# State-space stage: position-table products nine planner ticks sooner, and each table sent out in eight pieces from SyncE's queue

## The chip, the cores and the metric

The kernel runs on one core of a Trainium2 chip. The metric is the device time of one launch in microseconds (us); the number that counts is the median of the runs. One further execution is profiled, and all rows of the trace come from that one.

## The reference

Two transformer-like blocks over a sequence of 512 positions with 1024 features. The first has a state-space mixer (32 heads in 4 groups, scan in chunks of 128), convolutional feed-forward layers, and a differential attention with a learned bias by distance. The second has three mixed branches (one of them a sliding-window attention with its own bias table), a cross-attention and a feed-forward layer. The parts that the change touches are the two bias tables, which depend on nothing but the parameters:

```python
bias = rel_bias[t5_bucket(dist)].astype(jnp.float32).transpose(2, 0, 1)
logits = logits + bias[None, :, None]                 # first block, 8 heads
...
bias = rel_bias.astype(jnp.float32)[t5_bucket_2(dist)]  # second block, 8 heads
```

and the state-space mixer, beside which they are built:

```python
y_diag = jnp.einsum('bcgls,bgrcls,bcsgrp->bclgrp', cb, decay_in, xc)
states = jnp.einsum('bclgn,bgrcl,bclgrp->bcgrpn', bc, decay_states, xc)
y_off = jnp.einsum('bclgn,bcgrpn,bgrcl->bclgrp', cc, states_in, jnp.exp(a_cs))
```

## The kernel before

**Main work.** Nearly all time is matrix products with features on the partitions: 512 positions are the moving side, blocks of 128x128 weights the stationary one. Each product is made of three passes over a high and a low part (`features`, L1162). A group of output features takes one of the PSUM banks 0 to 2 in turn and is a row of pieces, two chunks of 128 inputs (six matmuls) each.

**The planner.** `Plan` writes the order of everything. One piece of main work is one tick; there are 1598. `self.start(name, key)` notes the tick at which a step begins; each engine's program runs through the ticks and, for each, issues what stands at `T - age`. So an engine's order is fixed; the engines run apart and are held together by semaphores alone. `self.once(name, key, test, windows)` starts a step at the first tick at which `test` holds and `place(windows)` finds banks: a window is (key, age, ticks), and each gets the lowest of the banks 3 to 7 that is free in these ticks. Taking a bank on TensorE (`take`) waits until the bank's former user has been read out.

**Weights.** A unit of 1024 columns (512 KB) is loaded by SyncE (`load`, L2746), split by ScalarE (`split`, the copy 128x1024 of L1562), cut by VectorE (`cut`, L2027, 128x1024), then used by TensorE. There are three buffers (`N_W`), so SyncE's load of a unit waits for the cut of the unit three earlier. In this stage one load is issued every four ticks.

**State-space stage.** For each of four groups `g`: `in` products with a convolution (VectorE's three L2030 of 128x512 each), `sta` (transposes `bt`, scores `scb`), `stb` (transposes `xc(g,c)` at ticks 0 to 3 of it, states `st(g,c)` at 7, 9, 11, two ticks of bank each), and four `pair` steps three ticks apart: `s0`, `s1`, then ScalarE's Relu and Exp on them, GpSimd's product, `bo` and `by`. ScalarE copies `st(g,0)` out one tick after it; `st(g,1)` and `st(g,2)` are added by VectorE. Group 0 has `sta` at tick 30, `stb` at 40, `pair` at 50, 53, 56, 59; group 1 has `stb` at 67 and `pair` from 77. `dec` at tick 19 prepares decays: `d1`, `d2` (bank 3, ticks 26 to 30), `d3` (bank 4, 30 to 32). `yn` of group 0 (tick 86) writes `Y0` over the memory in which the table inputs and tables lie, so it waits until these have gone out.

**The tables.** Rule `tabs`: it starts one tick after the end of `("in", 0, 5)`, tick 29. It makes four products `tb 0` to `tb 3`, five ticks apart (bank windows of five ticks; banks 5, 3, 3, 3), each of 8 rows by 320 columns, the last by 64 (L1271 to L1276). VectorE subtracts each from a mask two ticks later (L2206 to L2210) into `tabs[0]` (`tab1`, 640 columns) and `tabs[1]` (`tab2`, 384 columns), on 8 partitions. ScalarE then issues one DMA for each to HBM (L1671 to L1675), each row 128 times over: 8 x 128 x 640 and 8 x 128 x 384 floats, at ticks 37 and 57. Their readers (`tb` and `tb2`, SyncE) come hundreds of ticks later. Banks otherwise: `xc(0,0..3)` have 4, 5, 6, 7; `st(0,0)` 4, `st(0,1)` 3, `st(0,2)` 3; `st(1,0)`, `st(1,1)`, `st(1,2)` all 3; `s0(0,0)` 4, `s1(0,0)` 5.

Of the kernel before, what the change touches and what calls it, by code (L numbers as in the profile page):

```python
# [17 lines left out]
P = 128  # L18
# [22 lines left out]
L1, L2 = 640, 384  # L41
# [109 lines left out]
FIRST_ROW = 13  # L151
# [3 lines left out]
class Plan:  # L155
# [22 lines left out]
    def at(self, name, t):  # L178
        return self.starts.get(name, {}).get(t, ())
# [182 lines left out]
    def ssm(self):  # L362
# [5 lines left out]
        def first_row():  # L368
            if self.T >= FIRST_ROW and self.when("rms", "n1") is None:
                self.rms("n1")  # L370

        self.rules.append(first_row)
        self.once("tabs", 0, lambda: ("in", 0, 5) in self.end and self.T > self.end["in", 0, 5],
                  [(("tb", i), 5 * i, 5) for i in range(4)])
        self.once("dec", 0, lambda: ("dt",) in self.ev, [(("d1",), 1, 2), (("d2",), 7, 5), (("d3",), 11, 3)])
        silu = {}
# [615 lines left out]
class Kernel:  # L992
# [12 lines left out]
    def full(self, key):  # L1005
        return self.sig.bank[self.plan.bank[key]].full, self.turn(key)

    def empty(self, key):
        return self.sig.bank[self.plan.bank[key]].empty, self.turn(key)
# [545 lines left out]
def scalar_program(eng, K):  # L1555
    plan, buf, sig, dram = K.plan, K.buf, K.sig, K.dram
    at, full, empty, leave = plan.at, K.full, K.empty, K.leave
    w = Waits(eng)
# [83 lines left out]
    def ssm(T):  # L1642
        for key in at("conv", T - 1):
            _, g, i = key
# [10 lines left out]
        for key in at("conv", T - 3):  # L1655
            _, g, i = key
# [6 lines left out]
        for key in at("zsilu", T - 1):  # L1663
            _, g, i = key
# [3 lines left out]
            func(ACT.Tanh, buf.us[plan.u_n[key] % 3][:, 4:S + 4], buf.ZT[g % 2][:, i, :]).then_inc(*sig["tanh"].up(key))  # L1668
        for _ in at("once", T):
            eng.dma_start(buf.once[:, :], dram["once"]).then_inc(*sig.once.up())  # L1670
        for i, (name, ln, age) in enumerate((("tab1", L1, 8), ("tab2", L2, 28))):  # L1671
            for _ in at("tabs", T - age):
                w.wait_ge(*empty(("tb", 2 * i + 1)))
                eng.dma_start(dram[name], buf.tabs[i][:, 0:ln].unsqueeze(1).to_broadcast([8, P, ln])).then_inc(
                    *sig.tabs[i].up())  # L1675
        for _ in at("dec", T - 3):
            w.wait_ge(*sig["absn"].at())
            eng.add_instruction(mybir.InstLoadActFuncSet(name=eng.bass.get_next_instruction_name(), engine=eng.engine,
# [35 lines left out]
        for g, p in at("pair", T - 2):  # L1714
            n = 4 * g + p
            e_ = buf.ep[n % 2]
            for k in range(2):
                rows = slice(64 * k, 64 * k + 64)
# [20 lines left out]
        for i in range(4):  # L1739
            for g in at("yn", T - 1 - i):  # L1740
                h, _ = buf.operand(f"Y{g}", i)
                w.wait_ge(*sig["yn"].at(g, i))
                if g == 0:
                    w.wait_ge(*sig.tabs[0].at())
                    w.wait_ge(*sig.tabs[1].at())
                elif g == 1:
                    w.wait_ge(*full(("out", 0, 7)))
                else:
                    w.wait_ge(*full(("z", 3, 3)))
                copy(h, buf.XS[g % 2][:, i, :]).then_inc(*sig["hi"].up(f"Y{g}", i))  # L1750
# [984 lines left out]
def sync_program(eng, K):  # L2735
    plan, buf, sig, dram = K.plan, K.buf, K.sig, K.dram
    at = plan.at
    w = Waits(eng)

    def load(u):  # L2740
        if u >= len(plan.units):
            return
        off, n = K.offsets[u]
        if u >= N_W:
            w.wait_ge(*sig["cut"].at(u - N_W))
        eng.dma_start(buf.raws[u % N_W][:, 0:n], dram["w"][off:off + P * n].rearrange("(p n) -> p n", p=P)).then_inc(  # L2746
            *sig.w[u % N_W].up())

    for c in range(DC):
        if c % 2 == 0 and c // 2 < N_W:  # L2750
            load(c // 2)
        eng.dma_start(buf.x[:, c, :], dram["x"][c * P:c * P + P, :]).then_inc(*sig.x_in[c].up())
    load(N_W)
    eng.dma_start(buf.keep[:, :], dram["keep"]).then_inc(*sig.keep.up())
    n_gain = PAR["ssm_ln"][1]
    eng.dma_start(buf.par[:, n_gain:N_PAR], dram["par"][:, n_gain:N_PAR]).then_inc(*sig.par.up())
    load(N_W + 1)
    for T in range(plan.T):
        for u in plan.split_at.get(T, ()):
            load(u + N_W)  # L2760
        for h in at("tb", T):
            if h >= 2:
                w.wait_ge(*K.empty(("qk", h - 2, NT - 1, 1)))
            else:
                w.wait_ge(*K.full(("dn", 0, 1, DC - 1)))
            w.wait_ge(*sig.tabs[0].at())
            eng.dma_start(buf.tb[h % 2][:, :], skewed(dram["tab1"][h], L1, S)).then_inc(*sig.tb[h % 2].up())
        for c in at("reload", T):
            w.wait_ge(*sig.spill.at())
            w.wait_ge(*sig["msum"].at(c))  # L2770
            eng.dma_start(buf.x[:, c, :], dram["spill"][c * P:c * P + P, :]).then_inc(*sig.x_in[c].up())
        for tile in at("tb2", T):
            w.wait_ge(*sig.tabs[1].at())
            for half in range(2):
                q = 2 * (tile % 2) + half
                w.wait_ge(*(K.empty(("sqk", tile - 2, NT - 1, half)) if tile >= 2 else K.full(("dn", 1, 1, DC - 1))))
                eng.dma_start(buf.tb2[q][:, :], skewed(dram["tab2"][tile + 4 * half], L2, 256)).then_inc(*sig.tb2[q].up())
        for _ in at("end", T):
            for j in range(NT):
                w.wait_ge(*K.sig["fout"].at(j))  # L2780
                w.wait_ge(*K.sig["fout_d"].at(j))
                eng.dma_start(dram["out"][j * P:j * P + P, :], buf.tokens[:, j * D:j * D + D]).then_inc(*sig.out.up())
    w.wait_ge(*sig.out.at(NT))
# [97 lines left out]
```

## Time and profile before

| | us |
|---|---|
| median of 3 runs | 2407.59 (2406.8 to 2408.47) |
| profiled execution | 2408.69 |
| its span, first to last instruction | 2406.9 |
| TensorE busy | 2378.8 (99%) |
| VectorE busy | 1408.0 (59%) |
| ScalarE busy | 1052.7 (44%) |
| GpSimd busy | 369.7 (15%) |

How to read it: PE is TensorE (PEld its weight loads), DVE VectorE, ACT ScalarE, POOL GpSimd, SP SyncE; SPq and ACTq are DMA issues of these engines. Lines such as L1162 are those of small helpers that record every operation of a kind (L1162 matmul, L1166 transpose, L1562 ScalarE copy, L1565 ScalarE function, L2027 VectorE tensor-tensor, L2030 VectorE scalar-tensor-tensor), so an instruction is known by its shape and its place. Tiles are named t, banks bank. Arrows in brackets give the idle time ahead of an instruction and what ended it. All times count from the start of the span.

### The profile page before, as it was taken

To read this page: it belongs to the slowest core of one execution; us is meant where nothing else is said; L and a number is where in the kernel's file an instruction comes from. 1 tells how busy PE (TensorE), PEld (TensorE's weight loads), DVE (VectorE), ACT (ScalarE), POOL (GpSimd) and SP (SyncE) were. 2 spreads that over 40 slices of the span, in tenths; PEclk is the share of its full clock that TensorE was granted. 3 is DMA by queue.
4 is the path that set the end of the run, shared out by engine and by line. 5 is a ranking of instruction groups with operands and counts; after the bars stand their busy time and mean duration, and the time that the engine had idled before them with its cause. 6 is when DMAs were issued, how large, how long until landed. Compare 5 with 4: busy or idle time off the path is not lost.

```text
span 2406.9 us, 29799 instructions
## 1 busy us (share of the span) xinstructions
PE 2378.8 (99%) x11622; PEld 1933.8 (80%) x11622; DVE 1408.0 (59%) x2204; ACT 1052.7 (44%) x1805; POOL 369.7 (15%) x296
## 2 busy tenths in 40 slices
PE   8999999999999999999999999999999999999998
PEld 6677778888888877788888877787788887888887
DVE  6878776763666778766456557534565445443342
ACT  6654554442444677644234334324443334322223
POOL 0352252210111001121012100001211001110101
PEclk9999999999999999999999999999999999999999
DMA  4542223223223221232332332231243322223322
GB/s 164 105 97 79 79 66 101 97 86 107 97 82 119 80 71 52 72 105 92 99 101 89 99 130 71 79 101 62 66 131 128 113 97 88 89 94 103 101 82 85
DMA packets 74269, 226.21 MB, mean 94 GB/s; under 512 B 8080, under 2 KB 12304, under 8 KB 74000
## 3 DMA queue, kind: packets, MB, share of 16 engines
q1 hardware_dynamic: 69696, 215.90, 27.7%
q10 hardware_dynamic: 4432, 8.39, 2.0%
q8 instruction: 93, 1.52, 0.3%
q14 instruction: 48, 0.39, 0.1%
HBM read 215.87 MB, written 8.39 MB: 93 GB/s over the span
## 4 chain that ended last, share of the span: by engine, by line
PE 61%; DVE 1%; issue 0%; ACT 0%; POOL 0%; POOLq 0%; DVEq 0%
PE bank L1162 60%; PE bank L1166 1%; DVE t L2030 0%; DVE t L2027 0%; DVE t L2038 0%; ACT t L1562 0%; DVE t L2034 0%; POOL t L2597 0%; ACT t L1565 0%; POOLq L2816 0%; DVE t L2520 0%; DVEq L2816 0%; DVE t L2366 0%; DVE t L2526 0%; DVEq L771 0%
## 5 line engine op out<-in xcount | busy, mean ns | idle before, releaser
L1162 PE MATMUL bank<-t 128*128 128x512 f32 (+6 forms) x11196 | 2354.7, 376 | 18.4 <-DVE t L2030 8.7
L1162 PEld LDWEIGHTS bank<-t 128*128 128x128 f32 (+2 forms) x11196 | 1890.6, 185 | 451.5 <-issue 80.1
L1562 ACT ACTIVATE t<-t 128x1024 fp32r<-128x1024 f32 (+6 forms) x633 | 539.1, 862 | 636.7 <-PE bank L1162 275.3
L2027 DVE TENSOR_TENSOR t<-t 128x1024 fp32r<-128x1024 f32 (+6 forms) x686 | 625.7, 922 | 260.8 <-ACT t L1562 254.7
L1565 ACT ACTIVATE t<-t 128x512 f32<-128x512 f32 (+6 forms) x609 | 367.1, 617 | 460.5 <-DVE t L2027 304.0
L2597 POOL TENSOR_TENSOR t<-t 128x512 f32<-128x512 f32 (+4 forms) x216 | 328.9, 1528 | 1547.5 <-ACT t L1565 558.9
L2027 DVE TENSOR_TENSOR t<-bank,t 128x512 f32<-128x512 f32 (+4 forms) x411 | 276.1, 676 | 454.7 <-PE bank L1162 444.3
L2030 DVE SCALAR_TENSOR_TENSOR t<-t 128x512 f32<-128x512 f32 (+5 forms) x496 | 367.9, 751 | 103.2 <-ACT t L1565 63.0
L1562 ACT ACTIVATE t<-bank 128x512 f32<-128x512 f32 (+4 forms) x151 | 72.2, 498 | 167.1 <-PE bank L1166 145.2
L2600 POOL TENSOR_SCALAR t<-t 128x128 f32<-128x128 f32 (+3 forms) x64 | 40.1, 633 | 477.9 <-ACT t L1562 246.1
L2030 DVE SCALAR_TENSOR_TENSOR t<-bank,t 128x512 f32<-128x512 f32 x56 | 38.5, 688 | 68.9 <-PE bank L1162 68.9
L1166 PE MATMUL bank<-t 128*128 128x128 f32 (+1 forms) x426 | 67.6, 274 | 1.8 <-ACT t L1562 1.0
L1565 ACT ACTIVATE t<-bank,t 128x128 f32<-128x128 f32 (+1 forms) x144 | 42.4, 393 | 44.1 <-DVE t L2520 38.4
L2038 DVE CUSTOM_DVE_ANT_0 t<-bank,t 128x256 f32<-128x256 f32 (+3 forms) x128 | 55.7, 462 | 9.7 <-PE bank L1162 7.4
L1166 PEld LDWEIGHTS bank<-t 128*128 128x128 f32 (+1 forms) x426 | 49.7, 140 | 13.4 <-issue 3.9
L2030 DVE SCALAR_TENSOR_TENSOR t<-t,bank 128x512 f32<-128x512 f32 x40 | 28.4, 710 | 53.3 <-PE bank L1162 50.4
L1565 ACT ACTIVATE t<-bank 128x512 f32<-128x512 f32 (+3 forms) x73 | 38.5, 540 | 13.5 <-PE bank L1162 8.5
L2034 DVE TENSOR_SCALAR t<-t 128x256 f32<-128x256 f32 (+6 forms) x88 | 33.6, 383 | 2.9
L1562 ACT ACTIVATE t<-bank,t 128x256 f32<-128x256 f32 (+1 forms) x36 | 15.8, 495 | 25.6 <-PE bank L1162 23.9
L1565 ACT ACTIVATION_READ_ACCUMULATOR t<-t 128x1 f32 x128 | 24.4, 191 | 0.0
L1565 ACT ACT_TABLE_LOAD x12 | 15.4, 1283 | 0.2
L2038 DVE DVE_READ_ACCUMULATOR2_ANT t<- 128x1 f32 x128 | 10.6, 83 | 0.0
(29 smaller groups left out, 42.9 us busy)
## 6 DMA issues: line engine op xcount, KB each, us to landing
t<-in_w SPq DMA_DIRECT2D x304, 512.0 KB, 3.3
t<-in_w SPq DMA_DIRECT2D x48, 384.0 KB, 3.0
t<-in_w SPq DMA_DIRECT2D x56, 320.0 KB, 2.9
t<-in_w SPq DMA_DIRECT2D x28, 256.0 KB, 2.7
tab<-t ACTq DMA_DIRECT2D x1, 2560.0 KB
t<-in_x SPq DMA_DIRECT2D x8, 256.0 KB, 5.8
t<-tab SPq DMA_DIRECT2D x8, 256.0 KB, 3.6
spill<-t ACTq DMA_DIRECT2D x1, 2048.0 KB, 8.3
```

The source lines that it names most:

```text
L1162: return eng.matmul(out, lhs, rhs, start=start, stop=stop, skip_group_check=loose)
L1166: return eng.transpose(out, in_, ident[0:n, 0:n])
L1562: return eng.activation(out, in_, ACT.Copy, scale=scale)
L1565: return eng.activation(out, in_, f, bias=bias, scale=scale, accum_out=accum)
L2027: return eng.tensor_tensor(out, a, b, o)
L2030: return eng.scalar_tensor_tensor(out=out, in0=a, scalar=s, in1=b, op0=o0, op1=o1)
L2034: return eng.tensor_scalar(out, a, s0, None, o0)
L2038: return eng.tensor_tensor_reduce(out, a, b, 1.0, FMAX, ADD, MIN, m)
L2597: return eng.tensor_tensor(out, a, b, o)
L2600: return eng.tensor_scalar(out, a, s, s1, o, o1)
```

## The change

The rule `tabs` fires from tick 20 (`FIRST_ROW + 7`, `FIRST_ROW` being 13) instead of one tick after the end of `("in", 0, 5)`. ScalarE issues the tables no more; SyncE does, in its loop over ticks: `tab1` in eight pieces of 16 of the 128 copies at ages 8, 10, ..., 22 and `tab2` in eight at ages 24, 26, ..., 38, so at ticks 28 to 42 and 44 to 58. The pieces stand behind the weight load of the same tick and ahead of all else in SyncE's tick. Readers and `yn` wait for all eight pieces (`at(8)`).

```diff
-        self.once("tabs", 0, lambda: ("in", 0, 5) in self.end and self.T > self.end["in", 0, 5],
+        self.once("tabs", 0, lambda: self.T >= FIRST_ROW + 7,
                   [(("tb", i), 5 * i, 5) for i in range(4)])
...
-        for i, (name, ln, age) in enumerate((("tab1", L1, 8), ("tab2", L2, 28))):
-            for _ in at("tabs", T - age):
-                w.wait_ge(*empty(("tb", 2 * i + 1)))
-                eng.dma_start(dram[name], buf.tabs[i][:, 0:ln].unsqueeze(1).to_broadcast([8, P, ln])).then_inc(
-                    *sig.tabs[i].up())
...
-                    w.wait_ge(*sig.tabs[0].at())
-                    w.wait_ge(*sig.tabs[1].at())
+                    w.wait_ge(*sig.tabs[0].at(8))
+                    w.wait_ge(*sig.tabs[1].at(8))
...
         for u in plan.split_at.get(T, ()):
             load(u + N_W)
+        for q in range(8):
+            rows = slice(P // 8 * q, P // 8 * (q + 1))
+            for i, (name, ln, age) in enumerate((("tab1", L1, 8), ("tab2", L2, 24))):
+                for _ in at("tabs", T - age - 2 * q):
+                    w.wait_ge(*K.empty(("tb", 2 * i + 1)))
+                    eng.dma_start(dram[name][:, rows, :],
+                                  buf.tabs[i][:, 0:ln].unsqueeze(1).to_broadcast([8, P // 8, ln])).then_inc(
+                        *sig.tabs[i].up())
...
-            w.wait_ge(*sig.tabs[0].at())
+            w.wait_ge(*sig.tabs[0].at(8))
...
-            w.wait_ge(*sig.tabs[1].at())
+            w.wait_ge(*sig.tabs[1].at(8))
```

## Rows read from the trace of the kernel before

**Rows 1.** The page: busy time of each engine, share of the span, instructions.
```profile
PE 2378.8 (99%) x11622; PEld 1933.8 (80%) x11622; DVE 1408.0 (59%) x2204; ACT 1052.7 (44%) x1805; POOL 369.7 (15%) x296
```

**Rows 2.** Stretches: length; PE, PEld, DVE, ACT, POOL busy; granted clock, DMA share, GB/s.
```profile
80.00:100.00 20.00, 16.11 (x57) 10.82 (x55) 19.58 (x26) 10.71 (x20) 4.01 (x3) 0.91 0.57 103
...
88.00:92.00 4.00, 3.48 (x7) 2.15 (x8) 3.76 (x6) 2.67 (x4) 0.00 (x0) 0.57 0.70 180
```

**Rows 3.** Timeline of PE: start, length, instructions; in brackets idle time before, releaser.
```profile
53.86 0.66 PE L1166 MATMUL bank<-t 128*128 128x128 f32 x4 [0.46 <-DVE t L2027]
...
88.52 2.50 PE L1162 MATMUL bank<-t 128*128 128x512 f32 x3 [2.31 <-DVE t L2027]
...
99.80 1.46 PE L1162 MATMUL bank<-t 128*128 128x512 f32 x6 [1.48 <-ACT t L1565]
...
145.69 1.58 PE L1162 MATMUL bank<-t 128*128 128x512 f32 x4 [0.55 <-ACT t L1562]
```

**Rows 4.** Timeline of DVE: two of the four table subtractions, with a neighbour.
```profile
75.96 0.47 DVE L2027 TENSOR_TENSOR t<-t,bank 8x320 f32<-8x320 f32 x1
76.36 0.67 DVE L2027 TENSOR_TENSOR t<-bank,t 128x512 f32<-128x512 f32 x1
...
88.27 0.20 DVE L2027 TENSOR_TENSOR t<-t,bank 8x64 f32<-8x64 f32 x1
```

**Rows 5.** Timeline of ACT, ticks 48 to 52.
```profile
91.53 0.58 ACT L1562 ACTIVATE t<-bank 128x512 f32<-128x512 f32 x1
...
94.40 0.87 ACT L1565 ACTIVATE t<-bank,t 128x128 f32<-128x128 f32 x3
...
99.26 0.99 ACT L1565 ACTIVATE t<-bank 64x384 f32<-64x384 f32 x2
```

**Rows 6.** DMA views of 70 to 124 and 124 to 160 us: queue 10, weight loads' landing.
```profile
q10 hardware_dynamic: 1039, 2.63, 41.5%
...
t<-in_w SPq DMA_DIRECT2D x7, 512.0 KB, 16.7
...
q10 hardware_dynamic: 1025, 1.56, 35.7%
...
t<-in_w SPq DMA_DIRECT2D x5, 512.0 KB, 13.2
```

**Rows 7.** Stretch from 80 to 83 us, columns as in rows 2.
```profile
80.00:83.00 3.00, 3.00 (x15) 2.33 (x13) 2.93 (x5) 0.64 (x1) 1.00 (x1) 1.00 0.47 50
```

**Rows 8.** Single loads' landing at 0.7, 6.4, 61.9, 69.9 us; GB/s of 60 to 90; issue at 61.88.
```profile
t<-in_w SPq DMA_DIRECT2D x1, 256.0 KB, 2.8
...
t<-in_w SPq DMA_DIRECT2D x1, 256.0 KB, 6.3
...
t<-in_w SPq DMA_DIRECT2D x1, 512.0 KB, 3.2
...
t<-in_w SPq DMA_DIRECT2D x1, 512.0 KB, 19.6
...
GB/s 0 0 0 27 224 421 27 0 0 0 0 0 0 27 104 131 233 89 48 44 55 55 193 212 98 41 73 55 51 51 51 44 53 97 105 111 139 139 201 281
...
61.88 0.33 SPq L2746 DMA_DIRECT2D t<-in_w  x1
```

**Rows 9.** Timeline of ACT: splits of ticks 46, 54, 58, 70, copy of 75; DVE's tick 72.
```profile
89.55 1.06 ACT L1562 ACTIVATE t<-t 128x1024 fp32r<-128x1024 f32 x1 [0.94 <-DMA t<-in_w]
...
104.18 1.10 ACT L1562 ACTIVATE t<-t 128x1024 fp32r<-128x1024 f32 x1
...
112.89 1.04 ACT L1562 ACTIVATE t<-t 128x1024 fp32r<-128x1024 f32 x1
...
135.08 1.04 ACT L1562 ACTIVATE t<-t 128x1024 fp32r<-128x1024 f32 x1
...
137.70 4.72 DVE L2027 TENSOR_TENSOR t<-t 128x512 f32<-128x512 f32 x5
...
145.07 0.57 ACT L1562 ACTIVATE t<-bank 128x512 f32<-128x512 f32 x1
```

## The prediction

> **What bounds the kernel now.** Read the engine table and the slices of the page first: TensorE is busy for 2378.8 of 2406.9 us [rows 1], so a change pays only by idle TensorE time that it removes, and costs whatever idle time it adds. Then read the stretch that the change touches, the first group of the state-space stage. From 80 to 100 us TensorE is busy for 16.11 of 20 us, VectorE for 19.58, and the granted clock is 0.91; between 88 and 92 us it is 0.57, so part of that stretch ran at the lower level of 1.2 GHz [rows 2]. Last, read TensorE's idle gaps there: 0.46 us before 53.86, 2.31 before 88.52, 1.48 before 99.80, 0.55 before 145.69 [rows 3]. With the slow clock, (1 - 0.57) x 4 = 1.7 us, these 4.8 us are all that any change here could win: 6.5 us, 0.27%.
>
> By tick: the sequence of work on each engine follows the planner's ticks. TensorE reaches ticks 49, 53 and 76 at 88.52, 99.80 and 145.69 us. From tick 41 on VectorE is the late one, busy 19.58 of 20 us [rows 2]: while TensorE has finished tick 48, VectorE is at tick 45.
>
> **Part 1, the products nine ticks sooner.** The rule for the tables fired at tick 29; now it fires at tick 20, if banks are free. The table bank windows would be ticks 20-24, 25-29, 30-34 and 35-39. Banks 3 and 4 hold `d2` in ticks 26-30 and `d3` in 30-32, so by first fit the four products get banks 4, 4, 5, 3: the rule can fire. No other rule waits for it: `yn` of group 0 needs tick 77 by the tables, but tick 86 by its own `rms`, so the tick plan stays. The four products cost TensorE the same in either place. VectorE's subtractions (0.47 us for 320 columns, 0.20 for 64) [rows 4] leave ticks 31, 36, 41, 46 and go to 22, 27, 32, 37. The ones at 36 and 46, and the new one at 37, lie beside waits for ScalarE; 31 and 32 cancel. What is left on VectorE's busy stretch is the one at 75.96: the next instruction starts 0.40 us later, so VectorE and ScalarE run **0.4 us** earlier from there. The one at tick 27 stands ahead of the bank release that TensorE waits for at 53.86: up to +0.47 us on TensorE there, but TensorE has the lead until tick 49, so it costs nothing at the end.
>
> But the bank numbers of the next step change, and this is the first real effect. In the kernel before, `st(0,1)` (tick 49) takes bank 3 after the last table product, and the gap before 88.52 is that: VectorE's 8x64 subtraction ends at 88.47 [rows 4]. With the tables gone from ticks 40-48, the transposes `xc(0,0)` take bank 3 and `st(0,0)` (ticks 47, 48) takes it too; `st(0,1)` then gets the same bank and waits until ScalarE has copied `st(0,0)` out. That copy runs from 91.53 to 92.11 [rows 5], or to 91.7 with the 0.4 us. So the gap does not close, it grows: TensorE starts tick 49 at 91.7 and not 88.5, after 5.5 us of idleness (88.52 less 2.31: it ran dry at 86.2), and I expect the same slow clock after it. Then `s0(0,0)` of tick 50 comes at about 96.0 where ScalarE's work on it started at 94.40; those eight activations, one silu, a load of the function table and the first exponential [rows 5] follow, so that TensorE starts tick 53 at about 101 rather than 99.80. The same wait, one group later, is visible in the trace: `st(1,1)` shares its bank with `st(1,0)`, and TensorE waits 0.55 us for the copy at 145.07 [rows 3, 9]. Price of part 1 at tick 53: **+1 us** (bounds +0.3 without slow clock, +2 with it in full).
>
> **Part 2, the pieces on SyncE's queue.** Before, ScalarE issues each table as one DMA, at ticks 37 and 57 (2560 and 1536 KB). Queue 10 moved 2.63 MB from 70 to 124 us, and 1.56 MB from 124 to 157 [rows 6]: 49 and 48 GB/s. In a stretch with no weights the same 50 GB/s take a DMA share of 0.47 [rows 7]: about 8 of 16 engines, the eight partitions being the outermost extent. A piece keeps that extent of 8, so I keep the rate: a piece of tab1 (320 KB, 0.328 MB) takes 6.7 us, of tab2 (0.197 MB) 4.1 us. Weight loads share these engines: a load of 512 KB alone lands 3.2 us after its issue, with a burst of 421 GB/s, that is 1.3 us of the engines; beside the tables it landed after 16.7 and 13.2 us, 19.6 at worst [rows 6, 8]; one of ScalarE's waits for it was 0.94 us [rows 9].
>
> Now the pieces stand in the same queue as the weight loads. That such a queue is worked off in order shows at the start, where loads are issued faster than they move: 2.8 us to land for the first and 6.3 for one issued at 6.40 [rows 8]. SyncE waits at tick 28 for the second product's subtraction (VectorE, tick 27); the weight load of tick 29 stands behind that wait, but it waits for a later cut anyway (issued at 61.88), so this wait costs nothing. The one at tick 44 is long satisfied. Between two weight loads (every 4 ticks, 7 to 8 us) two pieces go in: 13.4 us of table work while tab1 goes out, 8.2 for tab2. So the queue gets behind. Piece 2 starts when the load of 61.88 is through, at 64.7. The load of tick 41 is behind six pieces: 64.7 + 6 x 6.7 = 104.9, with 1.3 for itself and 0.5 to signal: lands at 106.7 (before 103.9). The load of tick 45, behind one more of each kind: 117.5 (before 107.8). The load of tick 57, six tab2 pieces later: 142.2. These are the low values, in which the loads between take nothing from the tables; if every load stops the tables for 1 us more, they are 108.7, 120.5 and 148.2. Between, nearer neither end: **107.7, 119.0, 145.2**.
>
> Who waits: ScalarE's split of a load stands in its program order, and all behind it waits. The splits ran at 104.18, 112.89 and 135.08 [rows 9]. With part 1 the first is due at 105.2: it waits 2.5 us, and the exponentials behind it release TensorE's bank for tick 56 that much later, about +3 us. The second, then due near 116, waits 3 us; behind it are the factors for `by(0,3)` at tick 64, which had 1.5 us of slack: TensorE stands at about +3.6. The loads of ticks 49 and 53 are covered, since no pair runs and TensorE needs their cuts only later. The split at 135.08, due at 139, gets its load at 145.2; VectorE's sequence at 137.70 contains the cut behind it and ends at 148.6, not 142.42; after it come ScalarE's silu, one more split and the copy (145.07 before), for which TensorE waits at tick 76 [rows 9]: 151.5 instead of 145.69, **+5.9 us**. From there the tables are out and loads land in time; VectorE's waits in later ticks may give some tenths back and a slow clock after the new gaps may take 1.5, both left out. ScalarE loses two DMA issues (its queue only, nothing gained).
>
> **Sum.** +5.9, of which about 1 is part 1; I say **+6.0 us**. The profiled run took 2408.7 us with a span of 2406.9; the median shown is 2407.6, 1.1 below. The forecast is 2407.6 + 6.0 = **2413.6**.
>
> One rule of the Trainium skill speaks another way: "DMA: Bandwidth & Descriptors", section "Issuing engines are not separate DMA queues", has it that DMAs of several engines run on the same 16 and interleave, and that choosing among issuers saves only sequencer time. By it alone part 2 would leave the loads near their 14 to 18 us; it is the second rival. The same page, "Queues, rings and completion order", has each issuer's ring served in order and rings in turns, which is the forecast's mechanism; the 16.7 us beside the tables agree with turns.
>
> **The rivals.** (1) *Shallow backlog.* The rings drift apart, loads cost the tables nothing: landings 106.7, 117.5, 142.2. The waits are then 1.5, 2 and 3 us, partly inside slack: +2 to +4.5, about 2410.8. For it: 48.0 against 50 GB/s with and without weights beside. (2) *The queue does not matter.* Only part 1's bank wait is left, +0.3 to +2: 2408.6. Against it: the order at the start [rows 8]. (3) *Faster.* Pieces of 6.7 us let a load through after one piece where 16.7 us were usual, and TensorE passes tick 49 without the slow clock. It decides where a load finds at most one piece ahead; it would give the 1.7 us, the 1.48 and the rest of the gaps, -5 at most: 2402.6. Against it: two pieces per load, and the bank wait that grows. (4) *Deep backlog.* Gaps of 3 us or more at ticks 56 and 76 each bring the slow clock (1.5 us each), and each load stops the tables fully (148.2): +9 to +14, about 2419. (5) *Not as said:* the banks do not fit at tick 20, the pieces start later; part 2 stays, about the forecast's time.
>
> **How the numbers follow.** A difference below 0.2% (4.8 us) can't be told from none here. Chances: forecast with rival 5 0.46 (2411 to 2416.5; two thirds of it above 2412.4), shallow 0.25, queue indifferent 0.12, deep 0.13, faster 0.04. Slower by more than 0.2%: 0.31 + 0.13 + 0.06 for shallow's upper end and beyond = 0.50; faster 0.03; same 0.47. The likeliest case alone is 2411 to 2416.5; eight times in ten: 2407.0 to 2421.0, which leaves out faster, the best of indifferent and the worst of deep.
>
> **What would show it.** In the profile after: TensorE's gap before tick 49 ends by ScalarE's L1562 and lasts over 4 us (part 1 right) or vanishes (wrong). Issue to landing of the loads between 70 and 125 us: 18 to 27 us (forecast), at most 17 (rivals 2, 3). ScalarE waits for the DMA of `in_w` for over 2 us in each of several splits. Queue 1 carries all, the last piece is out by 155 us. A table rate of 100 GB/s, 16 engines on a piece, would make the whole of part 2 wrong, towards the second or third rival.

## The result, and the profile after

The changed kernel takes **2410.99 us** (median of 22 runs, 2408.39 to 2413.03) against 2407.52 (22 runs, 2406.75 to 2408.47): ratio 1.0014, 95% interval 1.0008 to 1.0019, +3.5 us. The forecast was 2413.6: the sign was right, the size 2.5 us too large. The run with the profile took 2410.38 us with a span of 2408.6.

The page's engine line, to set beside [rows 1]: TensorE is as busy as before to a tenth, in a span that is 1.7 us longer.

```profile
PE 2378.8 (99%) x11622; PEld 1935.4 (80%) x11622; DVE 1407.6 (58%) x2204; ACT 1053.3 (44%) x1805; POOL 367.5 (15%) x296
```

Stretches of the changed kernel, columns as in [rows 2]:

```profile
80.00:100.00 20.00, 14.15 (x47) 9.73 (x46) 16.91 (x21) 9.95 (x20) 4.00 (x3) 0.83 0.57 87
88.00:92.00 4.00, 1.62 (x3) 0.84 (x3) 3.96 (x5) 2.17 (x4) 1.04 (x1) 0.60 0.50 112
...
1408.00:1412.00 4.00, 4.00 (x22) 3.43 (x22) 2.04 (x7) 0.00 (x0) 0.00 (x0) 0.72 0.00 0
1412.00:1416.00 4.00, 4.00 (x20) 3.39 (x19) 0.00 (x0) 1.20 (x2) 0.00 (x0) 0.85 0.39 135
```

From 80 to 100 us TensorE is busy 2 us less than before and its clock is 0.83, not 0.91. The low level (1.2 GHz) lasts 6.8 us from 88.8 us, where it lasted 3.4 from 88.2 before. A second stretch of 3.4 us stands at 1409.8 us, in which this trace of the kernel before was at full clock.

The gaps of TensorE from its timeline (the answer to [rows 3]), and in the second block ScalarE's timeline, with its waits for weights (the answer to [rows 9]):

```profile
69.28 0.66 PE L1166 MATMUL bank<-t 128*128 128x128 f32 x4 [0.86 <-DVE t L2022]
...
90.38 35.95 PE L1162 MATMUL bank<-t 128*128 128x512 f32 x196 [5.85 <-ACT t L1562]
```
```profile
89.75 0.58 ACT L1562 ACTIVATE t<-bank 128x512 f32<-128x512 f32 x1
...
114.30 1.06 ACT L1562 ACTIVATE t<-t 128x1024 fp32r<-128x1024 f32 x1 [0.52 <-DMA t<-in_w]
...
122.59 1.06 ACT L1562 ACTIVATE t<-t 128x1024 fp32r<-128x1024 f32 x1 [1.91 <-DMA t<-in_w]
130.84 1.06 ACT L1562 ACTIVATE t<-t 128x1024 fp32r<-128x1024 f32 x1 [2.49 <-DMA t<-in_w]
139.03 1.06 ACT L1562 ACTIVATE t<-t 128x1024 fp32r<-128x1024 f32 x1 [3.56 <-DMA t<-in_w]
```

Read it so: one gap of 5.85 us before tick 49 took the place of 2.31 and 1.48, ended by ScalarE's copy of `st(0,0)`. The 0.86 us before 69.28 are new too: the transposes `xc(0,0)` take bank 3 right behind the last table product and wait for its subtraction; tick 47 is only 0.1 us late after them. The four waits for weights are there and grow, and yet no gap of TensorE stands behind them: 196 matmuls run on from 90.38, and the gap of 0.55 us before tick 76 is gone.

**A ruler for what follows.** All kernels issue the same products in the same ticks (but for the four table products, and the constants of experiments 10 and 12), so the start of tick N in one trace can be set against that in another. The start-up differs from run to run (tick 4 starts at 14.04 us in the kernel before, between 11.74 and 14.35 in the others), so shifts are counted from tick 4. "Tail" is the time from the last product to the end, against the kernel before; the last column is the median against that of the kernel before in the same series. A second profile was taken of either kernel. Where constants fill the idleness, the -2.4 at tick 49 is the first constant; the product `st(0,1)` behind them stands at +3.7 there.

| us later than before, from tick 4 on | tick 49 | 55 | 78 | 925 | 1500 | tail | median |
|---|---|---|---|---|---|---|---|
| before, again | 0.0 | 0.0 | 0.0 | 0.0 | 1.5 | 0.0 | |
| after | 3.7 | 2.1 | 1.3 | 1.3 | 2.8 | 0.6 | +3.5 |
| after, again | 3.7 | 2.2 | 2.0 | 2.2 | 2.2 | 0.6 | |
| products alone | 3.6 | 1.9 | 2.0 | 1.9 | 1.9 | 0.0 | +1.6 |
| pieces alone | 0.0 | 0.0 | 7.0 | 6.9 | 6.9 | 0.6 | +7.8 |
| after, other bank | -2.4 | 1.4 | 1.1 | 1.4 | 3.0 | 0.6 | +2.9 |
| after, pieces on ScalarE | 5.9 | 6.9 | 6.9 | 7.1 | 7.0 | 0.0 | +7.9 |
| before, other bank | -2.5 | 0.3 | 0.3 | 0.4 | 0.4 | 0.0 | +0.4 |
| products early, pieces late | 3.7 | 2.1 | 4.3 | 4.8 | 6.3 | 0.6 | +6.2 |
| pieces alone, from memory | 0.0 | 0.0 | 0.0 | 0.0 | 0.0 | 0.6 | +0.7 |
| after, idleness filled | -2.4 | 0.3 | 1.3 | 1.4 | 1.4 | 0.6 | +2.4 |
| after, ScalarE's stream refilled | 3.7 | 2.1 | 1.3 | 1.4 | 1.4 | 0.0 | +2.2 |
| all three causes removed | -2.4 | 0.3 | 0.4 | 0.5 | 2.1 | 0.0 | +0.9 |

A median of 11 runs is known to about 2 us in this comparison (the ratios' intervals are 0.0009 wide to either side; those of products alone, before with the other bank, pieces from memory, stream refilled and all three removed include 1), so what follows rests on the shifts and takes the medians as a rough sum.

The difference has four parts: 2.1 us by tick 55, of which 0.1 to 0.8 are given back by tick 78, 1.5 us between ticks 925 and 1500 in some runs, and 0.6 us in the tail.

### The profile page after: what moved, and what is told of

It is laid out like the page before. It is cut to its first block, busy times and chain, and to the rows that moved or that the text cites. A ratio compares the mean times of both kernels' runs of the same rounds, so it can differ in the third digit from the quotient of the medians.

```text
span 2408.6 us, 29813 instructions
## 1 busy us (share of the span) xinstructions
PE 2378.8 (99%) x11622; PEld 1935.4 (80%) x11622; DVE 1407.6 (58%) x2204; ACT 1053.3 (44%) x1805; POOL 367.5 (15%) x296
## 4 chain that ended last, share of the span: by engine, by line
PE 61%; DVE 1%; issue 0%; ACT 0%; POOL 0%; POOLq 0%; DVEq 0%
PE bank L1162 60%; PE bank L1166 1%; DVE t L2025 0%; DVE t L2022 0%; DVE t L2033 0%; ACT t L1562 0%; DVE t L2029 0%; POOL t L2592 0%; ACT t L1565 0%; POOLq L2819 0%; DVE t L2515 0%; DVEq L2819 0%; DVE t L2361 0%; DVE t L2521 0%; DVEq L771 0%
## 5 line engine op out<-in xcount | busy, mean ns | idle before, releaser
L1562 ACT ACTIVATE t<-t 128x1024 fp32r<-128x1024 f32 (+6 forms) x633 | 539.2, 862 | 643.7 <-PE bank L1162 274.2
L1562 ACT ACTIVATE t<-bank 128x512 f32<-128x512 f32 (+4 forms) x151 | 72.2, 498 | 168.6 <-PE bank L1166 146.8
L1562 ACT ACTIVATE t<-bank,t 128x256 f32<-128x256 f32 (+1 forms) x36 | 15.8, 495 | 25.6 <-PE bank L1162 23.9
```

Of the source, the lines that this page charges most:

```text
L1562: return eng.activation(out, in_, ACT.Copy, scale=scale)
```

## The experiments

**1. Products alone** (against the kernel before).

```diff
-        self.once("tabs", 0, lambda: ("in", 0, 5) in self.end and self.T > self.end["in", 0, 5],
+        self.once("tabs", 0, lambda: self.T >= FIRST_ROW + 7,
...
-        for i, (name, ln, age) in enumerate((("tab1", L1, 8), ("tab2", L2, 28))):
+        for i, (name, ln, age) in enumerate((("tab1", L1, 17), ("tab2", L2, 37))):
```

> The four table products at ticks 20 to 35 as in the changed kernel; the two tables go out as before, one DMA each on ScalarE's queue at ticks 37 and 57. Bank theory (the whole loss comes from st(0,1) sharing bank 3 with st(0,0), and from the slow clock after it): TensorE idles 5 to 6 us ahead of tick 49, ended by ScalarE's copy, and the median is 3 to 4 us above the kernel before, as with the full change. Queue theory (my prediction: late weight loads are most of it): only +1 us.

2409.06 us (11 runs), ratio 1.0007 [0.9998, 1.0016]. The gap before tick 49 is the changed kernel's, in place and length:

```profile
89.94 35.81 PE L1162 MATMUL bank<-t 128*128 128x512 f32 x196 [5.86 <-ACT t L1562]
...
145.41 4.79 PE L1162 MATMUL bank<-t 128*128 128x512 f32 x17 [0.55 <-ACT t L1562]
```

The shift by tick 55 is 1.9 us and it stays. That is the changed kernel's loss in the stage (1.3 and 2.0 us by tick 78), so on balance the pieces add nothing there. Neither theory had the size: the median is 1.6 us up, where one said 3 to 4 and the other 1.

**2. Pieces alone** (against the changed kernel).

```diff
-        self.once("tabs", 0, lambda: self.T >= FIRST_ROW + 7,
+        self.once("tabs", 0, lambda: ("in", 0, 5) in self.end and self.T > self.end["in", 0, 5],
```

> Products at tick 29 as before, so the banks are the old ones; the sixteen pieces go out on SyncE's queue at ticks 37 to 67. Bank theory: the gap ahead of tick 49 is 2 to 2.5 us as before, the median is within 1 us of the kernel before, though loads land 10 to 16 us after issue. Queue theory: +3 us or more, and ScalarE's waits for the loads show up as TensorE gaps near ticks 58 to 80.

2415.25 us (5 runs), ratio 1.0032 [1.002, 1.0045]. Timelines around tick 76, of ScalarE and then of TensorE:

```profile
139.00 1.06 ACT L1562 ACTIVATE t<-t 128x1024 fp32r<-128x1024 f32 x1 [4.68 <-DMA t<-in_w]
...
147.27 1.06 ACT L1562 ACTIVATE t<-t 128x1024 fp32r<-128x1024 f32 x1 [4.17 <-DMA t<-in_w]
148.23 0.58 ACT L1562 ACTIVATE t<-bank 128x512 f32<-128x512 f32 x1
```
```profile
148.87 3.35 PE L1162 MATMUL bank<-t 128*128 128x512 f32 x5 [4.61 <-ACT t L1562]
```

The chain is: late load, split, copy, TensorE at tick 76, which is 4.1 us late after a gap of 4.61 us; 6.8 us of low clock make it 7 us. It is not quite the one that the prediction priced. That one ran through the split of tick 70, which is the 139.00 here, and VectorE's cut behind it. This split was 4.8 us late against the kernel before (from tick 4 on) and the cut only 0.9, and then the cut was quicker. The kernel before, VectorE's cut and then GpSimd's product beside it:

```profile
140.11 2.31 DVE L2027 TENSOR_TENSOR t<-t 128x1024 fp32r<-128x1024 f32 x1
...
139.79 1.55 POOL L2597 TENSOR_TENSOR t<-t 128x512 f32<-128x512 f32 x1 [2.56 <-ACT t L1565]
```

The changed kernel:

```profile
140.40 1.22 DVE L2022 TENSOR_TENSOR t<-t 128x1024 fp32r<-128x1024 f32 x1
...
141.27 1.49 POOL L2592 TENSOR_TENSOR t<-t 128x512 f32<-128x512 f32 x1 [3.74 <-ACT t L1565]
```

Where ScalarE is late, GpSimd's product comes behind the cut and not beside it, and the cut takes 1.22 or 1.23 us, not 2.31. This holds in all 14 profiles: 2.31 us in the seven in which GpSimd's product starts 0.3 us ahead of the cut, 1.22 in the seven in which it starts 0.5 us or more after the cut's start. VectorE is then 0.2 us early with the pieces alone, and the 4.1 us are all of the next load, the one for the split at 147.27. So the chain exists, but the parts do not add: 1.6 and 7.8 us apart, 3.5 together.

**3. The change with another bank.** `st(0,1)` goes to bank 7, which is free in ticks 49 and 50 (against the changed kernel):

```diff
+            def other_bank(g=g):
+                if self.when("stb", g) == self.T and g == 0:
...
+                    self.bank["st", 0, 1] = 7
+                    self.taken[7] |= {self.T + 9, self.T + 10}
...
+            self.rules.append(other_bank)
```

> The changed kernel, but st(0,1) has bank 7, which has been free since tick 31. Bank theory: no gap ahead of tick 49; at most about 1 us ahead of tick 51 (st(0,2) still shares bank 3 with st(0,0)) and one ahead of tick 53; no slow clock there; the median is at the kernel before or up to 2 us below it. Queue theory: still +2.5 us or more.

2410.36 us (11 runs), ratio 1.0012 [1.0003, 1.0021]. TensorE's timeline:

```profile
90.77 3.89 PE L1169 MATMUL bank<-t 128*128 128x512 f32 x14 [1.39 <-ACT t L1569]
98.39 11.81 PE L1169 MATMUL bank<-t 128*128 128x512 f32 x59 [3.73 <-ACT t L1572]
```

The gap before tick 49 is gone and comes back before ticks 51 and 53, ended by ScalarE. Tick 53 then starts exactly when it did in the kernel before; 3.4 us of low clock behind it make 1.4 us by tick 55. The first expectation had the gap's move right and missed both this low clock and the time, 2.9 us above the kernel before instead of none. The bank chooses where TensorE idles. That it must idle is decided by VectorE and ScalarE.

**4. Pieces on ScalarE's queue.** The same 16 issues, in the changed kernel's ticks, in ScalarE's program.

> The changed kernel with the same sixteen pieces at the same ticks, but issued by ScalarE. In the changed kernel SyncE needed 3.8 to 4.9 us for an issue once earlier pieces were outstanding. If that is the issuing engine held up by its own full queue, ScalarE is now held up so, 10 or more times, in the middle of its work: TensorE gains gaps and the median is 15 us or more above the kernel before. If an issue is only slow on SyncE, or the hold-up costs ScalarE nothing, the median is that of the changed kernel, +3 to +4 us. Weight loads alone on SyncE's queue should then be issued in 0.3 us again, and land after 13 to 20 us.

2415.37 us (6 runs), ratio 1.0031 [1.002, 1.0042]. ScalarE's timeline, then TensorE's:

```profile
77.56 4.40 ACTq L1676 DMA_DIRECT2D tab<-t  x1
82.06 1.06 ACT L1562 ACTIVATE t<-t 128x1024 fp32r<-128x1024 f32 x1 [3.03 <-issue]
```
```profile
94.70 10.10 PE L1162 MATMUL bank<-t 128*128 128x512 f32 x30 [8.08 <-ACT t L1562]
```

SyncE's loads are issued in 0.33 us again, but a piece takes up to 4.4 us to issue while others are outstanding, now on the engine that TensorE waits for. The 7.9 us lie between the two expectations (3 to 4, and 15 or more).

**5, 6. Second profiles of both kernels.**

> The kernel before once more, for a second profile of it. Of its 23 executions beside the first four experiments, 18 had a mean granted clock of 0.999 (2406.6 to 2408.6 us) and 5 had 0.998 (2407.8 to 2408.5); the one whose trace the prediction read had 0.998 and took 2408.7. Theory A, that the trace read was an untypical one, with a low clock at tick 49 that most executions don't have: here no low clock between 80 and 110 us, a gap before tick 49 still near 2.3 us, a time near 2407.5. Theory B, that the low clock at tick 49 belongs to the kernel: again some 3.4 us of low clock from 88 us, and the time near 2408.5 or, if it is shorter, for a reason in the start-up.

> The changed kernel once more, for a second profile of it. Theory A: the gap before tick 49 is again 5.5 to 6 us and the low clock there again 6.8 us, whatever the rest does, and the time is 2410 to 2412; the second stretch of low clock near 1410 us (3.4 us, 1.6 us lost) is there or not, and with it the time is near 2411.5, without it near 2409.8. Theory B, that the second stretch is the change's doing: it is there again at the same place, tick 926.

They took 2408.22 and 2409.76 us. Stretches of the kernel before, second profile, and below them two of its first profile:

```profile
88.00:92.00 4.00, 2.78 (x12) 1.98 (x11) 3.96 (x6) 3.04 (x5) 1.04 (x1) 1.00 0.67 136
...
1408.00:1412.00 4.00, 4.00 (x15) 3.26 (x16) 2.04 (x7) 0.60 (x1) 0.00 (x0) 0.63 0.16 37
```
```profile
1408.00:1412.00 4.00, 4.00 (x32) 3.68 (x31) 1.71 (x7) 0.00 (x0) 0.00 (x0) 1.00 0.00 0
1412.00:1416.00 4.00, 4.00 (x23) 3.02 (x22) 0.91 (x2) 1.72 (x3) 0.00 (x0) 1.00 0.43 135
```

Theory A is half right. The low clock between 88 and 92 us, which the prediction counted as 1.7 us to be won, is absent here, and **nothing is gained by it**: every tick from 49 to 925 starts within 0.07 us of the first profile's, counted from tick 4. Inside tick 49 the products come up to 1.5 us sooner, and then TensorE waits in tick 50, whose `s0(0,0)` takes the bank of `st(0,0)`, for ScalarE's copy of that:

```profile
90.30 6.08 PE L1162 MATMUL bank<-t 128*128 128x512 f32 x22 [1.22 <-ACT t L1562]
```

In the first profile the slow products filled this wait. But theory A's time, 2407.5, was missed by 0.7 us: this run has a stretch of low clock at 1409 us, which does cost 1.5, and a start-up that is 2.0 us shorter. So that stretch is not the change's own: it is in the second profile of the kernel before and not in the second of the changed one. Of the 14 profiles of this study (the one of before that was read first among them) five have it, and each time it costs 1.5 to 1.6 us. TensorE is never idle there; in tick 926 it does 20 matmuls of 8 columns for the gate of the mixed branches, and the last of them ends 0.1 to 1.0 us before the clock falls. The nine other profiles have the same matmuls and no low clock, so they are not shown to be its cause.

**7. The kernel before with the other bank.** The same lines as in 3, on the kernel before.

> The kernel before, its tables untouched, with the second half of the first state (tick 49) on bank 7, so that it waits for no table product. If the bank wait costs what the gap shows: the 2.3 us before tick 49 go and with them 1 to 3 us of the time, 2405 to 2406.5. If the chain through VectorE and ScalarE behind it sets tick 53 anyway, as in the changed kernel with the other bank: the gap goes from tick 49 to ticks 51 and 53 (over 3 us before tick 53), tick 53 starts within 0.3 us of before, a low clock of 3.4 us comes behind tick 53 where most executions of before have none, and the time is 2407.5 to 2409.

2408.14 us (11 runs), ratio 1.0002 [0.9994, 1.0011]. The second answer holds, as to the mechanism, and its time too. The gap goes to tick 50 (3.34 us) rather than 51 and 53, the low clock lasts 6.8 us from 90.4, not 3.4, and tick 55 is only 0.3 us later.

**8. Products early, pieces late** (against the changed kernel).

```diff
-            for i, (name, ln, age) in enumerate((("tab1", L1, 8), ("tab2", L2, 24))):
+            for i, (name, ln, age) in enumerate((("tab1", L1, 17), ("tab2", L2, 33))):
```

> The changed kernel with its products where it has them (tick 20 on) and its pieces nine ticks later (ticks 37 to 67, as in the run with the pieces alone). If the pieces' start decides whether the queue hurts: landing of the loads of ticks 57 and 61 near 142.5 and 147, a gap of 3 to 5 us before tick 76, the cost of the products alone (+1.6) and of the pieces alone (+7.8) add up, less what the gap of tick 49 overlaps: 2414.5 to 2417. If it is the early products that protect the changed kernel: no gap before tick 76 and 2410 to 2412.

2413.98 us (9 runs), ratio 1.0026 [1.0016, 1.0036]. TensorE's timeline has the gap again, smaller:

```profile
148.04 7.99 PE L1162 MATMUL bank<-t 128*128 128x512 f32 x30 [2.70 <-ACT t L1562]
```

So it is the start of the pieces that protects the changed kernel, not its products. Against the pieces alone the gap is 1.9 us smaller, about the 2.1 us by which TensorE is late anyway: two delays on one path overlap, they don't add. No low clock follows this smaller gap, so tick 78 is 4.3 us late and not 7.0. This is why the expected 2414.5 was missed by 0.5 us.

**9. Pieces alone, copied from memory.** The first piece's tick writes one row (8 rows of the table), and all pieces are copied from there (against the kernel before):

```diff
...
+                    if q == 0:
+                        w.wait_ge(*K.empty(("tb", 2 * i + 1)))
+                        eng.dma_start(dram[name][:, 0, :], buf.tabs[i][:, 0:ln]).then_inc(*sig.tabs[i].up())
+                        w.wait_ge(*sig.tabs[i].at(1))
+                    eng.dma_start(dram[name][:, rows, :].rearrange("h r l -> r h l"),
+                                  dram[name][:, 0:1, :].to_broadcast([8, rows.stop - rows.start, ln])
+                                  .rearrange("h r l -> r h l")).then_inc(*sig.tabs[i].up())
...
```

> The pieces alone (products at tick 29, +7.8 us in the run before), but each table is first written once to memory (8 rows) and its pieces are then copied from that row, with 16 target rows outermost, instead of from 8 partitions. If a piece is slow because its source has 8 partitions (half of the 16 engines, 49 GB/s): a piece of tab1 takes 3.5 us or less instead of 6.6, the loads of ticks 49 to 61 land within 10 us, SyncE's issues are short, the gap before tick 76 is back at 0.55 us, and the time is 2407.5 to 2409. If it is slow by its bytes (2.5 KB packets, writes to memory), or if sharing SyncE's queue is itself the cost: landings and time as with the pieces alone, 2414 to 2416.

2408.35 us (11 runs), ratio 1.0002 [0.9993, 1.0011]. Landing of the loads in the changed kernel (70 to 124 us) and in this one (66 to 140 us):

```profile
t<-in_w SPq DMA_DIRECT2D x5, 512.0 KB, 13.4
```
```profile
t<-in_w SPq DMA_DIRECT2D x9, 512.0 KB, 3.3
```

SyncE's timeline, of the changed kernel and of this one:

```profile
79.24 8.29 SPq L2761 DMA_DIRECT2D tab<-t  x2
87.58 4.84 SPq L2741 DMA_DIRECT2D t<-in_w  x1
```
```profile
85.78 0.36 SPq L2741 DMA_DIRECT2D t<-in_w  x1
86.18 1.19 SPq L2764 DMA_DIRECT2D tab<-tab  x2
```

The same bytes in the same queue and ticks: loads land in 3.3 us, the 7 us in the stage are gone (0.00 us at tick 78), and what stays is the tail. The queue hurt only because a piece from 8 partitions holds it for 6.6 us. Source and outermost extent (8 before, 16 now) were changed together; which of them does it was not separated. The Trainium skill, "DMA: Bandwidth & Descriptors", section "Why a DMA increments its semaphore by 16 and not by 1", has it that the number of engines is the largest up to 16 that divides the slowest extent of both sides. That speaks for the extent, and the DMA share of 0.47 at 50 GB/s [rows 7] agrees.

**10. The idleness filled** (against the changed kernel).

```diff
+                if g == 0 and c == 1:
+                    spare = sig.bank[7]
+                    w.wait_ge(spare.empty, spare.n)
+                    for _ in range(20):
+                        mm(buf.banks[7][:, 0:P], tri, ones)
                 bank = take(("st", g, c))
```

> The changed kernel with 20 products of constants (128x128, fp32, about 0.27 us each, into a bank that nobody uses then) that TensorE works off while it waits before tick 49; nobody reads them. If the products' cost (some 2 us by tick 55) is the low clock that follows the 5.8 us of idleness: no low clock between 85 and 100 us, the idle time before tick 49 under 1 us with its start still near 90.4, tick 55 near its place in the kernel before, and 2408 to 2409.5 in all. If the chain through VectorE and ScalarE sets tick 53 whatever the clock: a gap of 2 to 3 us before tick 53 and the time of the changed kernel, 2410.5 to 2411.5.

2410.11 us (11 runs), ratio 1.0009 [1.0001, 1.0018]. A stretch, then TensorE's timeline, then ScalarE's:

```profile
88.00:92.00 4.00, 2.60 (x13) 1.71 (x11) 4.00 (x5) 2.67 (x4) 1.04 (x1) 1.00 0.50 101
```
```profile
89.88 12.06 PE L1162 MATMUL bank<-t 128*128 128x512 f32 x50 [1.40 <-ACT t L1567]
...
102.36 2.68 PE L1162 MATMUL bank<-t 128*64 128x128 f32 x22 [0.43 <-POOL t L2597]
...
144.71 5.68 PE L1162 MATMUL bank<-t 128*128 128x512 f32 x20 [1.01 <-ACT t L1567]
```
```profile
138.63 1.06 ACT L1567 ACTIVATE t<-t 128x1024 fp32r<-128x1024 f32 x1 [4.72 <-DMA t<-in_w]
```

The clock stays at 2.4 GHz and tick 55 is 0.3 us late instead of 2.1: **1.8 us of part 1 is the low clock** behind the bank wait, and 0.3 stays, with a gap of 0.43 us that GpSimd ends. But the median's distance falls by only 1.1 us. With TensorE earlier, ScalarE's wait at tick 70 grows from 3.56 to 4.72 us, the next split waits another 0.37, and a gap of 1.01 opens before tick 76. The late loads were there all the time, under the delay of tick 49. The expected 2408 to 2409.5 was missed for that, and for the tail.

**11. ScalarE's stream refilled.** Eight waits that are already met, where the two transfers left (against the changed kernel).

```diff
+        for i, age in ((0, 8), (1, 28)):
+            for _ in at("tabs", T - age):
+                for _ in range(4):
+                    eng.wait_ge(*empty(("tb", 2 * i + 1)))
```

> The changed kernel with eight waits that are already met on ScalarE, in place of the two transfers that left its stream. In all five profiles where the pieces are on SyncE's queue the time from the last product to the end is 0.6 us longer than in the five others, and an 8 KB fetch of instructions stands 2.5 us before the end, inside the last output transfers, where it stood 9.1 us (or over 20) before the end otherwise. If this is ScalarE's code, shorter by some instructions: with the waits the fetch moves ahead of the outputs and the tail is 0.6 us shorter, everything before it as in the changed kernel; 2410 to 2410.8. If it is SyncE's queue or its 16 transfers: the tail stays 0.6 us longer, 2410.5 to 2411.5.

2409.90 us (11 runs), ratio 1.0007 [0.9998, 1.0016], 0.1 us below what was expected. SyncE's last wait, in the kernel before, the changed one and this one:

```profile
SPq L2816 <- DMA out<-t: 3.7, 1, 3.7
```
```profile
SPq L2819 <- DMA out<-t: 4.3, 1, 4.3
```
```profile
SPq L2823 <- DMA out<-t: 3.7, 1, 3.7
```

The queues in the last 5 to 6 us, in the same order (packets, MB, share of 16 engines):

```profile
q1 hardware_dynamic: 454, 1.60, 81.0%
```
```profile
q1 hardware_dynamic: 345, 1.22, 61.9%
q14 instruction: 1, 0.01, 0.4%
```
```profile
q1 hardware_dynamic: 468, 1.66, 69.7%
```

With eight idle instructions the fetch of 8 KB of code (q14) leaves the output transfers, and the last of them lands 0.6 us sooner; up to tick 925 the trace is the changed kernel's to 0.1 us. ScalarE's program had become shorter, and a fetch that stood 9.1 us before the end slid to 2.5 us before it. That the fetch holds up one engine's share of the outputs is inferred; that the 0.6 us come and go with its place shows in all 14 profiles (seven have it in the last 2.7 us and are 0.6 us longer, seven have it at least 9.0 us before the end and are not).

**12. All three removed.** The edits of 9, 10 and 11 on the changed kernel.

> The changed kernel with three things at once: its pieces copied from a row in memory (no queue backlog), TensorE's idleness before tick 49 filled with constants, eight met waits in ScalarE's stream. If the causes found are all there are and add up (stage: +0.3 us by tick 55 as with the idleness filled, then nothing more at tick 76, where that kernel lost 1.0; tail 0.0 against 0.6): the last product 0.3 to 0.5 us later than before from tick 4 on, and the time 2407.5 to 2408.5. If something else of the change costs time: over 2409.

2408.20 us (11 runs), ratio 1.0002 [0.9993, 1.0011]. Tick 55 is 0.3 us late, no gap stands before tick 76 beyond that of the kernel before, the tail is 0.0. The last product came 2.1 us late in the profiled run and not 0.3 to 0.5, because of the stretch at 1410 us (1.5 us); the median is within the expected range. So with the three causes gone the stage and the tail are back to within 0.5 us; what is left of the median, 0.9 us against that of its own series, is within the noise of the comparison. Neither this nor any other kernel here beats the kernel before.

## Why the prediction was right in sign and too large

That the sign and the stated range held is in good part luck. Of the +6.0 us, 4.9 were the pieces, which on balance cost nothing in the stage; of the +3.5 measured, the part that was forecast with the right cause, the bank wait, was put at 1 and is about 2, and the rest, the tail and the stretch at 1410 us, stands in no term.

*The bound of what can be won.* Wrong: the 1.7 us of slow clock between 88 and 92 us were counted as idle time to be regained, also in the rival that forecasts faster. The second profile of the kernel before shows that they cost nothing, for TensorE waits in tick 50 for ScalarE anyway. The Trainium skill, "TensorE: Matmul & The Clock Gate", section "Terms", puts the penalty at the throttled time times one half. It measured 0.0 us for the 3.4 there and 1.8 for the 6.8 of the changed kernel; for the stretch at 1410 us, where TensorE is never idle, 1.5 for 3.4, near the 1.7 that the rule would give.

*Part 1, banks 4, 4, 5, 3 and the bank wait.* Right: the gap before tick 49 is ended by L1562 and lasts 5.85 us (5.5 forecast). The copy that ends it was to end at 91.7, with 0.4 us gained on VectorE; in the clock of the kernel before (1.79 us for the earlier tick 4) it started at 91.54, where [rows 5] have 91.53, and ended at 92.1. The 0.4 us were gained at 75.96, but they only made good what VectorE and ScalarE had lost before: behind the subtraction of tick 27 both run 0.4 us late. Mis-sized: "+1 us at tick 53, bounds +0.3 to +2"; measured +2.7 at tick 53 and +2.1 at tick 55, of which 1.8 is low clock (experiment 10). The prediction took the slow clock after the new gap to be the same as before; the longer gap brought twice as much.

*The product at tick 27.* Priced at up to 0.47 us, costing nothing at the end. Right for TensorE, whose tick 30 is 0.6 us late and tick 47 only 0.1; the price on VectorE, the 0.4 us above, was left out.

*Part 2, rate of a piece.* Right: 6.6 and 4.1 us (6.7 and 4.1 forecast), from loads that landed every 13.25 us and then every 8.2.

*Part 2, landings.* The step that failed first. Forecast 107.7, 119.0, 145.2, with 106.7, 117.5, 142.2 as the lowest; measured, in the clock of the kernel before, 105.3, 116.1 and 140.8. All three are 1.4 us under the lower end: each load lands with the end of the pieces ahead of it, and the 1.8 us for the load itself and its signal, added in the forecast, do not show (the first piece counts from 65.7, a load's landing, and not from 64.7, and the pieces are a little shorter; together that is the 1.4). The choice of the middle value added another 1.0, 1.5 and 3.0 us.

*Part 2, who waits.* The step that failed most. The prediction had ScalarE wait 2.5 us at tick 54, 3 at tick 58 and 6.2 at tick 70, and all of it arrive at TensorE by tick 76, +5.9. Measured: 0, 0.52 and 3.56 us, and TensorE without a gap. The split of tick 70 was to pass its delay on through VectorE's cut. Its load landed at 140.8 in the clock of the kernel before, the split ended at 141.9, and VectorE, late by part 1, came to the cut at 142.2: nothing was passed on, and the cut was 1.1 us quicker for GpSimd's later product (experiment 2). Landings that are 4.4 us too late (145.2) and no look at this slack made the 5.9 us. What can reach TensorE is the load behind it, which had no price of its own. With the pieces alone it costs 4.1 us at tick 76, and 7 with the slow clock; with the pieces nine ticks sooner it comes 3.7 us sooner (143.52 against 147.25 us; 2.8 counted from tick 4). In the first profile ScalarE does not wait for it; in the second it does, for 0.82 us, and a gap of 0.39 us stands before tick 76:

```profile
144.40 1.06 ACT L1562 ACTIVATE t<-t 128x1024 fp32r<-128x1024 f32 x1 [0.82 <-DMA t<-in_w]
...
145.99 17.92 PE L1162 MATMUL bank<-t 128*128 128x512 f32 x94 [0.39 <-ACT t L1562]
```

That is why the first has 1.3 us at tick 78 and the second 2.0. With part 1's low clock gone (experiment 10) the loads cost 1.0 us there; otherwise that lies under part 1's delay. The prediction added part 2 to part 1 as if they stood one behind the other; they are two delays on one path, and the longer counts.

*"ScalarE loses two DMA issues (its queue only, nothing gained)".* Wrong: it cost 0.6 us in the tail.

*The profile's signs.* Issue to landing at most 17 us was to speak for the rivals in which the queue does not matter. The median was 13.4, yet the queue did matter: SyncE itself was held up to 4.9 us at an issue, so a late load shows as a late issue. The interval between landings was the sign to name. The 100 GB/s that would have made part 2 wrong did not show.

*The rivals.* "Shallow backlog", 2410.8 us, gives the measured time, and its landings are the nearest, though still 1.4 us too late. Its mechanism is not what happened: its 2 to 4.5 us were waits of ScalarE that reach TensorE. "The queue does not matter", 2408.6, is nearest to what the stage shows of the full change (+1.3 to +2.2 us), for a reason it did not have. The rule of the Trainium skill's "DMA: Bandwidth & Descriptors", section "Issuing engines are not separate DMA queues", that choosing among issuers saves only sequencer time, is not what the runs show: loads on SyncE are issued in 0.33 us when the pieces are on ScalarE, and the stage is lost to ScalarE's held issues instead.

*The sum.* Forecast: 1.0 + 4.9. Measured: 1.3 to 2.2 us in the stage, 0.6 in the tail, 1.5 at 1410 us in some runs; +3.5 in the median.

**Open.** Whether the changed kernel meets the stretch at 1410 us more often than the kernel before. Stage and tail give 1.9 to 2.8 us, the median says 3.5; "after, other bank", "pieces on ScalarE", "products early, pieces late" and "stream refilled" are also 0.8 to 0.9 us over their sums, the others at most 0.4. Fourteen profiles are too few to tell, and nothing here moved that stretch on purpose. The sums also leave out the start-up, which differs by up to 2.6 us from run to run and is known for the profiled runs alone; that it is longer in some kernels than in others is not excluded. Nor was it tested alone that the cut's 2.31 us are GpSimd's doing.

## What to carry to other kernels

Ask of every added wait which other delay already covers the same ticks, and take the longer, not the sum; then ask what appears once the cover goes, for it was found here only by removing the larger. A transfer's time in a shared queue is set by its shape: a small piece from few partitions holds everything behind it, and a compact copy in memory, with 16 rows outermost, cost one more hop and freed the queue. What a late wait on one engine costs depends on how soon the next engine wants the result: look up that slack before you pass a delay on. Count a stretch of low clock only where TensorE is what the next step waits for.

## What the runs showed of the hardware that was not expected

- A DMA issue takes 0.33 us on an idle queue and mostly 3.8 to 4.9 us on SyncE, up to 4.4 on ScalarE, while several slow pieces are outstanding in the same queue.
- A weight load behind pieces costs them nothing measurable: landings every 13.25 us for two pieces and a load between, where two pieces alone would take 13.1 us at the 50 GB/s of [rows 7] (an estimate).
- With one fetch of 8 KB of code inside the last output transfers the kernel is 0.6 us longer, and eight idle instructions more or less in one engine's program decide it.
- The clock fell at 1410 us, where TensorE was never idle, in 5 of 14 profiles, and that cost 1.5 to 1.6 us.
- A cut of 128x1024 on VectorE took 2.31 us beside a product of GpSimd (seven profiles) and 1.22 us where that came later (seven).
